# Delta-rule tile of a hybrid decoder step: state products behind the inversion, decay matrix on ScalarE from repeated gate rows

## The reference, cut to what matters

```python
gcum = jnp.cumsum(gc, axis=-1)
decay = jnp.exp(jnp.where(tri, gcum[..., :, None] - gcum[..., None, :], -jnp.inf))
kb = kc * bc[..., None]
a = jnp.where(strict, jnp.einsum('nbhid,nbhjd->nbhij', kb, kc) * decay, 0.0)
rhs = jnp.concatenate([vc * bc[..., None], kb * jnp.exp(gcum)[..., None]], axis=-1)
sol = lax.linalg.triangular_solve(a + eye, rhs, left_side=True, lower=True, unit_diagonal=True)
u, w = sol[..., :DV], sol[..., DV:]
qk = jnp.einsum('nbhid,nbhjd->nbhij', qc, kc) * decay
def step(S, inp):
    q_i, k_i, u_i, w_i, qk_i, g_i = inp
    v_new = u_i - jnp.einsum('bhck,bhkv->bhcv', w_i, S)
    o_i = (jnp.einsum('bhck,bhkv->bhcv', q_i * jnp.exp(g_i)[..., None], S)
           + jnp.einsum('bhij,bhjv->bhiv', qk_i, v_new))
    g_last = g_i[..., -1]
    S = (S * jnp.exp(g_last)[..., None, None]
         + jnp.einsum('bhck,bhcv->bhkv', k_i * jnp.exp(g_last[..., None] - g_i)[..., None], v_new))
    return S, o_i
```

## Time and profile before

| what | us |
|---|---|
| median of 3 runs | 2296.68 |
| lowest and highest of them | 2290.75, 2300.85 |
| the profiled execution's own time | 2300.1 |
| its span in the profile | 2298.3 |
| tile loop, from the first k transpose (434.8) to the last tile's output product (993) | 558.2 |
| one tile in it | 68.3 to 70.7 |

### The profile page before, as it was taken

One profiled execution on the slowest core, in us unless ns is written; L12 is line 12 of the kernel. 1 busy time (PEld: TensorE's weight loads), 2 busy tenths in 40 slices (PEclk: granted clock), 3 DMA queues, 4 the chain that ended last, 5 costly groups with the idle time before them and its releaser, 6 DMA issues.

```text
span 2298.3 us, 36017 instructions
## 1 busy us (share of the span) xinstructions
PE 2139.2 (93%) x13767; PEld 2077.7 (90%) x13767; DVE 984.2 (43%) x1678; ACT 528.8 (23%) x1125; POOL 780.1 (34%) x342
## 2 busy tenths in 40 slices
PE   4999998699999999989989989679999999999996
PEld 4999997599898889989969989579999999999996
DVE  5555034444444434420235850654334334334336
ACT  4332153233333333321112221420000000000003
POOL 2434446321111221112214434434444444444444
PEclk9999999899999999999879989789999999999998
DMA  4323322421222321134265423221111111111113
GB/s 149 93 84 103 93 84 96 122 80 33 82 77 73 82 73 38 50 106 151 78 197 172 157 65 107 98 67 37 55 46 37 55 46 37 55 46 37 55 37 151
DMA packets 225201, 189.54 MB, mean 82 GB/s; under 512 B 24619, under 2 KB 200299, under 8 KB 225090
## 3 DMA queue, kind: packets, MB, share of 16 engines
q1 hardware_dynamic: 213202, 179.63, 25.4%
q10 hardware_dynamic: 11904, 8.52, 1.2%
HBM read 142.07 MB, written 47.06 MB: 82 GB/s over the span
## 4 chain that ended last, share of the span: by engine, by line
PE 85%; DVE 6%; ACT 3%; issue 2%; DMA 1%; POOL 1%; SPq 1%; POOLq 0%; DVEq 0%; ACTq 0%
PE psum L1268 22%; PE psum L838 14%; PE psum L1048 12%; PE psum L1335 10%; PE psum L917 6%; PE psum L1260 5%; PE psum L1278 4%; PE psum L1033 2%; PE psum L1022 1%; PE psum L1006 1%; DVE xs L2223 1%; PE psum L1011 1%; ACT pr L1585 1%; PE psum L1129 1%; DVE asm L1987 1%
## 5 line engine op out<-in xcount | busy, mean ns | idle before, releaser
L738 POOL TENSOR_TENSOR wsp<-raw,kc 128x1024 fp32r<-128x1024 f32 x145 | 349.4, 2410 | 1410.0 <-PE psum L1048 455.9
L1268 PE MATMUL psum<-actD,wsp 128*128 128x352 f32 x3168 | 514.5, 322 | 0.9 <-DVE actD L2229 0.9
L1268 PEld LDWEIGHTS psum<-actD,wsp 128*128 128x128 f32 x3168 | 508.6, 189 | 1.0 <-DVE actD L2229 1.0
L741 POOL TENSOR_TENSOR wsp<-raw,wsp 128x1024 fp32r<-128x1024 f32 x145 | 364.3, 2512 | 11.4
L838 PE MATMUL psum<-actT,wsp 128*128 128x352 f32 (+1 forms) x1944 | 315.9, 324 | 0.0
L838 PEld LDWEIGHTS psum<-actT,wsp 128*128 128x128 f32 (+1 forms) x1944 | 307.7, 186 | 5.2
L1048 PE MATMUL psum<-actT,wsp 128*128 128x352 f32 x1728 | 302.6, 332 | 0.0
L1048 PEld LDWEIGHTS psum<-actT,wsp 128*128 128x128 f32 x1728 | 284.8, 194 | 0.1
L2278 DVE TENSOR_TENSOR accT<-accT,psum 128x352 f32<-128x352 f32 x504 | 242.3, 520 | 50.4 <-PE psum L1335 50.4
L1335 PE MATMUL psum<-fT,wsp 128*128 128x352 f32 x1512 | 250.4, 323 | 0.4 <-DVE accT L2278 0.4
L1335 PEld LDWEIGHTS psum<-fT,wsp 128*128 128x128 f32 x1512 | 244.5, 188 | 0.7 <-DVE accT L2278 0.7
(11 more groups left out here) (387 smaller groups left out, 2315.4 us busy)
## 6 DMA issues: line engine op xcount, KB each, us to landing
raw<-in_w_in SPq DMA_DIRECT2D x100, 256.0 KB, 3.9
raw<-in_w_ffn_in SPq DMA_DIRECT2D x88, 256.0 KB, 3.1
gat<-s_gate SPq DMA_DIRECT2D x12, 1056.0 KB, 5.0
raw<-in_w_ffn_out SPq DMA_DIRECT2D x44, 256.0 KB, 2.7
s_gate<-gst SPq DMA_DIRECT2D x48, 176.0 KB, 1.9
s_qkv<-y SPq DMA_DIRECT2D x12, 528.0 KB, 3.0
brw<-s_br SPq DMA_DIRECT2D x3, 2112.0 KB, 9.7
raw<-in_w_branch SPq DMA_DIRECT2D x24, 256.0 KB, 6.2
```

The costliest lines, as they stand in the source:

```text
L738: pool.tensor_tensor(wsp[:, slot, 0], raw[:, slot], ones.unsqueeze(1).to_broadcast([P, KT, P]), ALU.mult).then_inc(w_hi, 1)
L741: pool.tensor_tensor(wsp[:, slot, 1], raw[:, slot], wsp[:, slot, 0].bitcast(F32), ALU.subtract).then_inc(w_lo, 1)
L1268: mm = pe.matmul(psum[:, bank, 0:CH], wsp[:, slot, a, k, :], actD[:, h, k, CH * c:CH * c + CH], start=(k == 0 and q == 0), stop=(k == KT - ...
```

## The change

The delta rule becomes v_new = X·(vb − bke·(k·S)): the product of k with the state (`KS`) is made when the inversion's last step has been issued, DVE scales it and subtracts it from `vb` in place, and one product with X (`UN`) gives v_new, which ACT copies from bank 6 to `vn`. The products `UW` and `wt`·`st`, the tensors `kbe`, `ug`, `bi`, `uu`, `wt`, and their copies go. In `TILE`, `KS` and `PO` (now only q with `st`, into bank 7) stand right behind X 6, ahead of S 4, and `UN` behind G 3.

The decay matrix comes from two rows for each tile and head, gcum and beta times norm factor. Ahead of the loop PE transposes them to 32 rows, ACT copies them, SP stores them to `s_row` in HBM, and for each tile SP loads its rows back repeated on all 128 partitions (`rowb`, 512 KB in SBUF). ACT takes, for each head, Relu of (the token's own gcum minus the row) into `dec`, waits for the four, and takes exp of the negative in place. DVE multiplies `at` by the second row. `load_rows(t + 1)` stands in SP's queue behind the second gate store of tile t.

```diff
-            ("S", 4), ("D", 0), "UW", ("G", 3), ("F", 0), "PO", ("T", 4), ("V", 4), ("S", 5), "SO", ("T", 5),
+            "KS", "PO", ("S", 4), ("D", 0), ("G", 3), "UN", ("F", 0), ("T", 4), ("V", 4), ("S", 5), "SO", ("T", 5),
...
+                    if j == 0 and c == 1 and not last:
+                        sp.wait_ge(at_st, 4 * t + 2)
+                        load_rows(t + 1)
...
+        sp.wait_ge(rw_cp, 2)
+        for x in range(2):
+            sp.dma_start(s_row[x].rearrange("t (h i) -> (t h) i", h=BH), rowt[:, x, :]).then_inc(rw_st, 16)
         sp.sem_inc(c_ob, 1)
+
+        def load_rows(t):
+
+            sp.dma_start(rowb[:].rearrange("p x h i -> p x (h i)"),
+                         s_row[:, bass.ds(t, 1), :].rearrange("x a n -> (a x) n").partition_broadcast(P)).then_inc(rw_in, 16)
+
         for s in range(2):
             load_gate(s, (NPB + s) % 2)
         load_tile(0, 0)
+        sp.wait_ge(rw_st, 32)
+        load_rows(0)
...
-                pool.tensor_tensor(ug[:], bc_h(k_le), bc_c(per(Q_G, t)), ALU.mult).then_inc(ug_ok, 1)
                 pool.tensor_tensor(mrk[:], bc_h(k_le), bc_c(per(Q_RK, t)), ALU.mult).then_inc(mrk_ok, 1)
-                pool.wait_ge(kq_ok, t + 1)
-                pool.tensor_tensor(bi[:], bc_h(ident), bc_c(per(Q_BK, t)), ALU.mult).then_inc(bi_ok, 1)
...
-                elif step == "DEC":
-                    pe.wait_ge(ug_ok, t + 1)
-                    pe.wait_ge(c_s, t + 1)
-                    pe.matmul(psum[:, 7, :], k_gt, ug[:], start=True, stop=True).then_inc(e_gt, 1)
-                    pe.wait_ge(bi_ok, t + 1)
-                    pe.wait_ge(kd_ok, t + 1)
-                    pe.matmul(psum[:, 5, :], ones, bi[:], start=True, stop=True).then_inc(e_br, 1)
...
+                elif step == "KS":
+                    pe.wait_ge(c_x, 6 * t + 6)
+                    pe.wait_ge(c_s, t + 1)
+                    mm4(5, k, lambda h: st[:, h, :], e_ks)
...
-                elif step == "UW":
+                elif step == "PO":
                     pe.wait_ge(c_xt, 6 * t + 6)
+                    mm4(7, q, lambda h: st[:, h, :], e_o1)
+                elif step == "UN":
+                    pe.wait_ge(c_xt, 6 * t + 6)
+                    pe.wait_ge(r_ok, t + 1)
                     mm4(6, lambda h: xt[:, h, :], lambda h: vb[:, h, :], e_u)
-                    mm4(5, lambda h: kbe[:, h, :], lambda h: xt[:, h, :], e_w)
-                elif step == "PO":
-                    pe.wait_ge(c_w, t + 1)
-                    mm4(7, lambda h: wt[:, h, :], lambda h: st[:, h, :], e_p1)
-                    mm4(5, q, lambda h: st[:, h, :], e_o1)
...
-                    act.wait_ge(e_gt, t + 1)
+                    act.wait_ge(rw_in, 16 * t + 16)
                     act.wait_ge(dm_ok, t + 1)
-                    act.activation(dec[:].rearrange("p h i -> p (h i)"), psum[:, 7, :], ACT.Exp).then_inc(dec_ok, 1)
+                    for h in range(BH):
+                        mm = act.activation(dec[:, h, :], rowb[:, 0, h, :], ACT.Relu, scale=-1.0,
+                                            bias=gcm[:, bass.ds(t, 1), h])
+                    mm.then_inc(dec_ok, 1)
+                    act.wait_ge(dec_ok, 2 * t + 1)
+                    act.activation(dec[:].rearrange("p h i -> p (h i)"), dec[:].rearrange("p h i -> p (h i)"), ACT.Exp,
+                                   scale=-1.0).then_inc(dec_ok, 1)
...
-                elif step == "UW":
-                    copy((e_u, t + 1), uu[:].rearrange("p h i -> p (h i)"), psum[:, 6, :], c_u)
-                    copy((e_w, t + 1), wt[:].rearrange("p h i -> p (h i)"), psum[:, 5, :], c_w)
+                elif step == "UN":
+                    copy((e_u, t + 1), vn[:].rearrange("p h i -> p (h i)"), psum[:, 6, :], vn_ok)
...
-                    dve.tensor_tensor(kbe[:], head4(5), bc_c(per(Q_BKE, t)), ALU.mult)
...
-                    dve.tensor_tensor(at[:], at[:], head4(5), ALU.mult).then_inc(at_st, 1)
+                    dve.tensor_tensor(at[:], at[:], rowb[:, 1], ALU.mult).then_inc(at_st, 1)
...
+                elif step == "KS":
+                    dve.wait_ge(e_ks, t + 1)
+                    dve.tensor_tensor(ks[:], head4(5), bc_c(per(Q_BKE, t)), ALU.mult).then_inc(ks_ok, 1)
+                    dve.wait_ge(ks_ok, t + 1)
+                    dve.tensor_tensor(vb[:], vb[:], ks[:], ALU.subtract).then_inc(r_ok, 1)
                 elif step == "PO":
-                    dve.wait_ge(c_u, t + 1)
-                    dve.wait_ge(e_p1, t + 1)
-                    dve.tensor_tensor(vn[:], uu[:], head4(7), ALU.subtract).then_inc(vn_ok, 1)
```

More of the change, by code:

```diff
@@ L110, in build @@
     s_br = dram("s_br", [12, P, N])
+    s_row = dram("s_row", [2, NT, BH * P])
     psum = ctx.enter_context(nc.psum_tensor("psum", [P, 8, 512], F32))
@@ L129, in build @@
     egl = sb("egl", [P, NT + 1, BH])
+    gcm = sb("gcm", [P, NT, BH])
     tmp = sb("tmp", [P, 6, NT + 1, BH])
@@ L220, in build @@
     Q_BETA, Q_G, Q_BK, Q_BKE, Q_KD, Q_EG, Q_RK, Q_RQ = range(8)
-    vb, kbe, kd = (sb(n, [P, BH, P], on=cC) for n in ("vb", "kbe", "kd"))
-    ug, bi, mrk = (sb(n, [P, BH, P], on=cC) for n in ("ug", "bi", "mrk"))
+    vb, kd = (sb(n, [P, BH, P], on=cC) for n in ("vb", "kd"))
+    rowb = sb("rowb", [P, 2, BH, P], on=cC)
+    rowt = sb("rowt", [BH * NT, 2, P], on=cC)
+    mrk = sb("mrk", [P, BH, P], on=cC)
     dec, decm, kqd, at = (sb(n, [P, BH, P], on=cC) for n in ("dec", "decm", "kqd", "at"))
@@ L226, in build @@
     vn = sb("vn", [P, BH, P], on=cC)
-    uu, wt = xx, yy
+    ks = yy
     o1s, oo = (sb(n, [P, BH, P], on=cC) for n in ("o1s", "oo"))
@@ L247, in build @@
     c_sm = sem("c_sm")
-    ug_ok, bi_ok, mrk_ok = sem("ug_ok"), sem("bi_ok"), sem("mrk_ok")
-    e_tk, e_tv, e_gt, e_br, e_kk, e_kq, e_x0, e_y, e_xx, e_xt, e_u, e_w, e_p1, e_o1, e_sp, e_o2, e_ot = (
-        sem("e_" + n) for n in "tk tv gt br kk kq x0 y xx xt u w p1 o1 sp o2 ot".split())
+    mrk_ok = sem("mrk_ok")
+    rw_mm, rw_cp, rw_st, rw_in, ks_ok, r_ok = (sem(n) for n in "rw_mm rw_cp rw_st rw_in ks_ok r_ok".split())
+    e_tk, e_tv, e_kk, e_kq, e_ks, e_x0, e_y, e_xx, e_xt, e_u, e_o1, e_sp, e_o2, e_ot = (
+        sem("e_" + n) for n in "tk tv kk kq ks x0 y xx xt u o1 sp o2 ot".split())
     kd_ok, vb_ok, dec_ok, dm_ok, kq_ok, at_st, al_ok = (sem(n) for n in "kd_ok vb_ok dec_ok dm_ok kq_ok at_st al_ok".split())
-    c_x, c_xt, c_y, c_u, c_w, vn_ok, c_o1, c_o, c_s, c_ob = (
-        sem(n) for n in "c_x c_xt c_y c_u c_w vn_ok c_o1 c_o c_s c_ob".split())
+    c_x, c_xt, c_y, vn_ok, c_o1, c_o, c_s, c_ob = (
+        sem(n) for n in "c_x c_xt c_y vn_ok c_o1 c_o c_s c_ob".split())
     o_st1, o_sq, o_rt, on_ok = sem("o_st1"), sem("o_sq"), sem("o_rt"), sem("on_ok")
@@ L908, in _ @@
                 mm.then_inc(mt, 1)
+        pe.wait_ge(pp, 15)
+        pe.wait_ge(rw_cp, 1)
+        pe.transpose(psum[0:BH * NT, 7, 0:P], gcm[:].rearrange("p t h -> p (t h)"), ident)
+        pe.transpose(psum[0:BH * NT, 7, P:2 * P], par[:, Q_BK, 0:NT, :].rearrange("p t h -> p (t h)"), ident).then_inc(rw_mm, 1)
         pe.wait_ge(mc, 1 + 4)
@@ L912, in _ @@
         pe.wait_ge(qz_ok, 2)
+        pe.wait_ge(rw_cp, 2)
         def mm4(bank, lhs, rhs, done, w=P):
@@ L976, in pe_tile @@
                     pe.wait_ge(c_y, 6 * t + l)
-                    if l == 1:
-                        pe.wait_ge(kq_ok, t + 2)
-                    else:
+                    if l > 1:
                         pe.wait_ge(c_xt, 6 * t + l - 1)
@@ L1528, in _ @@
                     act.activation(dst[0:NS, NT, :], psum[0:NS, 5, 36 * x + 32:36 * x + 36], ACT.Exp).then_inc(pa, 1)
+                act.activation(gcm[:], psum[:, 5, 0:32].rearrange("p (t h) -> p t h", h=BH), ACT.Copy).then_inc(rw_cp, 1)
                 act.wait_ge(pp, 11)
@@ L1535, in _ @@
                 act.activation(mout[:, s, :] if v == 0 else mv[:, s, :], psum[:, 5 + j % 2, :], ACT.Copy).then_inc(mc, 1)
+        act.wait_ge(rw_mm, 1)
+        act.activation(rowt[:].rearrange("n x i -> n (x i)"), psum[0:BH * NT, 7, 0:2 * P], ACT.Copy).then_inc(rw_cp, 1)
         for c in range(3):
@@ L1915, in dve_tile @@
                 elif step == "DEC":
-                    dve.wait_ge(dec_ok, t + 1)
+                    dve.wait_ge(dec_ok, 2 * t + 2)
                     dve.wait_ge(mrk_ok, t + 1)
@@ L1938, in dve_tile @@
                             dve.tensor_tensor(atl[:, l - 1], at[:], m, ALU.mult).then_inc(al_ok, 1)
+                elif step == "KS":
[3 more added lines that the diff above has]
+                    dve.tensor_tensor(vb[:], vb[:], ks[:], ALU.subtract).then_inc(r_ok, 1)
                 elif step == "PO":
-                    dve.wait_ge(c_u, t + 1)
-                    dve.wait_ge(e_p1, t + 1)
-                    dve.tensor_tensor(vn[:], uu[:], head4(7), ALU.subtract).then_inc(vn_ok, 1)
                     dve.wait_ge(e_o1, t + 1)
                     dve.wait_ge(c_o, t + 1)
-                    dve.tensor_tensor(o1s[:], head4(5), bc_c(per(Q_EG, t)), ALU.mult).then_inc(c_o1, 1)
```

(1 more changed line is left out.)

7 lines of the change are left out of this document (4 added, 3 removed).

## The result

The changed kernel takes 2314.1 us (median of 6 runs, 2309.8 to 2318.9) against 2297.9 for the kernel before on the same chip: a ratio of 1.0065, 95% interval 1.0051 to 1.0080. It is slower by 0.65%, 16 us. The prediction said 2301.3 and a range to 2310.0, so the time lies outside the range, on the side of the rivals 2 and 3.

What follows compares the result with a forecast made beforehand. The DVE chain ahead of S 1, behind ACT's decay, was taken as the bound at a tile's head; 8 x (0.74 - 0.25) + 0.7 = +4.6 us gave 2301.3 us against the 2296.7 median, range 2293 to 2310 (own range 2298 to 2306).

Steps and rivals of the forecast that it cites:

- What bounds a tile: Head of the tile: DVE's chain up to V 0's copy sets S 1's start; PE's 2.0 us gained become a wait.
- Rival 1: Whole loop: PE is the bound after all, so work leaving its queue gains 23 us, giving 2273; chance 0.07.
- the Relus' duration: Head, on ACT: four Relus 0.20 apart, the last 0.30 long, then Exp, so decm starts 0.74 us later.
- the full 0.30: Head, on ACT: upper bound of the distance between Relus, making decm 1.04 us later instead of 0.74.
- rival 2: Head, on ACT: Relus take 0.41 each without overlap, decm 1.48 us later, sum +10.5, giving 2307; chance 0.12.
- The 0.2 us from kbe: Head: kbe leaving DVE lets S 0's maxima start at 647.24, not 647.48, and ACT's exponentials 0.2 us earlier.
- The tail: Behind the inversion: PE gains about 1.0 us, ACT's queue takes three quarters, V 4 starts 0.25 us earlier.
- Ahead of the loop: Before tile 0: SP's two row stores delay the gate loads, costing +0.7 us once.
- that transfer is hidden: In the loop: load_rows is issued some 35 us before ACT wants it, so its 512 KB cost nothing.
- rival 3: Tile heads: PE's new idles lower the clock, costing 1.5 us eight times, sum +16.6, giving 2313.3; chance 0.06.

Runs made afterwards that it cites:

- the decay alone: Changed kernel with the delta rule of the kernel before (kbe, u and w, vn = u - w S) and the new decay; 2310.2 us, ratio 1.0059 to before.
- the second profile: The changed kernel run again unaltered on the same chip, profiled anew; 2312.4 us against 2299.6 before, ratio 1.0051, loop 564.9 or 565.8 us.

## Why the prediction was wrong

**What bounds a tile: right.** The DVE chain in front of S 1 decides, and PE's freed time becomes a wait. decm moved by +1.33 in the changed kernel and +1.35 with the decay alone against before, and by -2.2 with the decay ahead of the exponentials and -1.3 without Relus against the changed kernel, and the head by the same each time. PE's busy time fell by 2.4 in tile 3 (2 to 3 forecast), its waits ahead of INV and S 1 are 2.25 and 1.44 (1.6 and 1.5 forecast), released by the operations named. Rival 1 is out.

**The step that failed: the Relus' duration.** I took a distance of 0.20 from two small ACT operations, and 0.90 for the four. They take 1.27: with 1.27 = 3 x distance + 0.394 (the mean of one in the groups by line) the distance is 0.29. The bound that I called "the full 0.30" was the measured value; but I had put the last Relu's own length at 0.30, as the squares', and it is 0.39. The step to Exp and Exp itself are 1.97 from the first Relu to decm (653.73 - 651.76) where I had 1.57 (650.67 - 649.10): 0.37 of the 0.40 is the Relus, 0.03 the Exp from SBUF. A row with a pointer operand stood in the same chain: the exponential of 128x256, 0.47 long, and the line through it and 128x512 that rival 2 drew gave 0.41 for one. That is close to the measured 0.394. Rival 2, to which I gave 0.12, named the right mechanism and size for one; it erred in letting the four not overlap (1.64 in place of 1.27). Its sum, 2307, still came out low, since it shared the two terms below.

The Trainium skill, page "ScalarE: Activation LUTs", section "Rules for kernel authors", had budgeted about 0.3 us an ACTIVATE with a pointer bias and 0.83 ns an element, an estimate of 1.6 us for the four. Measured are 0.394 for one, near the 0.41 of that estimate, and 1.27 for four back to back: this budget is right for one alone, and four times it is too high for a row of them.

**The 0.2 us from kbe: lost in the tiles with a split.** kbe's leaving does bring S 0's maxima to PE's pace; they are released by PE at 649.74. But the small operation behind them took 0.35 in place of 0.16, and ended at 650.82 as POOL's split ended (648.44 + 2.36 = 650.80). In the tiles 2 and 6, in which POOL doesn't run a split there, the gain is had: the head is 13.01 in place of 13.19. In tile 3 S 0's exponentials so begin 3.54 behind the tile's first weight load, where they began at 3.55 (648.39 - 644.84). The gain was eaten by a neighbour that the earlier start ran into: 0.74 forecast, plus 0.4 and 0.2, is the 1.33 measured. The decay alone, which keeps kbe, has that head (13.20) in all tiles behind the first.

**The tail: +0.04 in place of -0.25.** I followed ACT's queue and not the PSUM bank that F 0 and T 4 share. The two state products between them had been cover for the oba copy, and they are what moved away. T 4 waits 0.98 for it (rows of the tail, above). DVE's oat was in time, as forecast (697.72 + 0.69, F 0's load at 698.88), with 0.5 to spare.

**Ahead of the loop: +1.0 in place of +0.7.** From ACT's last mv copy to the first k transpose it is 15.2 where it was 14.2. The two row stores are 0.80 together, and the first repeated load 1.13; the timeline of the changed kernel there:

```profile
421.85 0.80 SPq L558 DMA_DIRECT2D s_row<-rowt  x2
...
430.59 1.13 SPq L563 DMA_DIRECT2D rowb<-s_row  x1
...
434.01 1.96 PE L947 MATMUL psum<-kc,gin 128*128 128x128 f32 x8 [14.99 <-POOL qz L783]
```

In the loop no Relu waited for its rows; that transfer is hidden, as forecast.

**The clock: dismissed too lightly.** I wrote that 4.0 us of idle in tile 3's window at a clock of 1.00 spoke against rival 3. Loop pauses of some 2 us are followed by the 1.2 GHz level in some tile heads, of the kernel before too, and the new waits added a stretch at that level in four tiles, 0.1 to 0.7 us each (V 0 to X 1). Rival 3 is right in kind, and its price is 1.1 us over the loop against before and not 12; that the result is near its 2313.3 is chance.

**The sum again, by what was measured:** 8 x (1.33 + 0.04) + 1.0 = +12.0. The loop's own difference is 10.2 (one tile already had a slow head before) and 9.3 in the second profile, with 1.0 ahead of it. The medians differ by 16 and 13. The 2.5 to 5 us that remain are not explained: the granted clock over the profiled execution was 0.951 for the changed kernel and 0.961 before, the stage behind the loop varies by more than that between executions, and the decay alone shows +12 in its median with that stage at its usual length. Whether the change lowers the clock there or two profiles happened to meet it was not settled.
